# Three score buffers and a longer pipeline in a sliding-window attention stage: P turned two steps and mixed three steps behind the scores

## The reference, cut to what matters

```python
def block_fn(args):                      # one block of 128 queries, keys of this and the previous block
    n, qb, kb, vb = args
    s = jnp.einsum('bqkgd,bskd->bkgqs', qb.astype(f32), kb.astype(f32)) * scale
    valid = band & ((n - 1) * BLOCK + kj >= 0)
    s = jnp.where(valid, s, -jnp.inf)
    m = jnp.maximum(jnp.max(s, axis=-1), sink)
    p = jnp.exp(s - m[..., None])
    denom = jnp.sum(p, axis=-1) + jnp.exp(sink - m)
    o = jnp.einsum('bkgqs,bskd->bqkgd', p / denom[..., None], vb.astype(f32))
    return o.astype(hn.dtype)
...
return o @ w_o + b_o                     # then h = h + this
```

## Time and profile before

| what | value |
|---|---|
| three runs, median | 1072.28 us (1071.91 to 1072.68) |
| the profiled execution | 1071.9 us |
| its span, first to last instruction | 1070.1 us |
| busy over the span | PE 96%, DVE 55%, ACT 21%, POOL 66% |
| chain that ended last | PE 84%, DVE 8%, issue 3%, ACT 2% |
| attention, scores(0) to the last mix | 579 to 679 us |

### The profile page before, as it was taken

The page is one execution under the profiler, slowest core; times in us unless marked ns, Lnnn a source line. Parts: engine busy times, 40 slices in busy tenths (PEclk is TensorE's granted clock), DMA queues, the critical chain, the costliest instruction groups (busy, mean ns, idle before and its releaser), DMA issues.

```text
span 1070.1 us, 15713 instructions
## 1 busy us (share of the span) xinstructions
PE 1032.4 (96%) x5734; PEld 847.5 (79%) x5734; DVE 585.5 (55%) x688; ACT 224.0 (21%) x489; POOL 702.1 (66%) x563
## 2 busy tenths in 40 slices
PE   4889999999999999999999998999999999999996
PEld 1778888888888888888888676888888888888886
DVE  7998246587515613722865787478771372174125
ACT  4673211111000000100321777321110010010011
POOL 7997776597766766766656230488776676676660
PEclk9699999999999999999999999999999999999998
DMA  6113332222322222222222110132322222232212
GB/s 244 28 32 100 107 111 98 85 99 99 99 98 99 98 98 95 90 97 96 94 99 84 55 40 21 40 118 99 104 95 98 98 98 98 99 98 99 98 59 79
DMA packets 35888, 97.52 MB, mean 91 GB/s; under 512 B 11136, under 2 KB 13696, under 8 KB 35584
## 3 DMA queue, kind: packets, MB, share of 16 engines
q1 hardware_dynamic: 35840, 96.85, 27.3%
HBM read 92.37 MB, written 2.10 MB: 88 GB/s over the span
## 4 chain that ended last, share of the span: by engine, by line
PE 84%; DVE 8%; issue 3%; ACT 2%; POOL 1%; DMA 1%; DVEq 0%; SPq 0%
PE ps L1162 24%; PE ps L1163 23%; PE ps L1164 23%; PE ps L1126 2%; PE ps L1128 2%; PE ps L1127 2%; PE ps L1303 1%; PE ps L1317 1%; PE ps L1291 1%; ACT s_sb L597 1%; PE ps L1225 1%; PE ps L1224 1%; PE ps L1223 1%; DMA prm<-prm_in 1%; DVE hid L827 0%
## 5 line engine op out<-in xcount | busy, mean ns | idle before, releaser
L420 POOL TENSOR_TENSOR w_lo<-raw,w_hi 128x1024 fp32r<-128x1024 f32 x164 | 414.8, 2529 | 13.7
L1162 PE MATMUL ps<-hid,w_hi 128*128 128x512 f32 x704 | 275.8, 392 | 0.0
L1163 PE MATMUL ps<-hid,w_hi 128*128 128x512 f32 x704 | 274.0, 389 | 0.0
L1164 PE MATMUL ps<-hid,w_lo 128*128 128x512 f32 x704 | 274.0, 389 | 0.0
L344 POOL TENSOR_TENSOR gate_sb<-gate_sb 128x1 f32<-128x1 f32 x164 | 40.2, 245 | 315.9 <-PE ps L1164 276.3
L1162 PE MATMUL ps<-act,w_hi 128*128 128x512 f32 x464 | 180.6, 389 | 0.0
L1164 PE MATMUL ps<-act,w_lo 128*128 128x512 f32 x464 | 180.5, 389 | 0.0
L1163 PE MATMUL ps<-act,w_hi 128*128 128x512 f32 x464 | 180.5, 389 | 0.0
L417 POOL TENSOR_SCALAR w_hi<-raw 128x1024 fp32r<-128x1024 f32 x164 | 172.7, 1053 | 0.0
L1162 PEld LDWEIGHTS ps<-hid,w_hi 128*128 128x128 f32 x704 | 132.1, 188 | 30.9 <-issue 3.2
L1164 PEld LDWEIGHTS ps<-hid,w_lo 128*128 128x128 f32 x704 | 132.2, 188 | 27.7
(11 more groups left out here) (211 smaller groups left out, 1097.5 us busy)
## 6 DMA issues: line engine op xcount, KB each, us to landing
raw<-panels_in SPq DMA_DIRECT2D x164, 512.0 KB, 3.3
xy<-xu_in SPq DMA_DIRECT2D x4, 512.0 KB, 7.6
out<-h SPq DMA_DIRECT2D x8, 256.0 KB, 2.2
prm<-prm_in SPq DMA_DIRECT2D x1, 1280.0 KB, 5.5
h<-x_rows_in SPq DMA_DIRECT2D x1, 1280.0 KB, 13.2
h<-x_rows_in SPq DMA_DIRECT2D x1, 768.0 KB, 7.8
dd<-dd_in SPq DMA_DIRECT2D x1, 256.0 KB, 5.8
toep<-k_even SPq DMA_DIRECT2D x4, 64.0 KB, 2.3
```

The costliest lines, as they stand in the source:

```text
L420: nc.gpsimd.tensor_tensor(w_lo[:, s, :], raw[:, s % 2, :], w_hi[:, s, :].bitcast(F32), ALU.subtract).then_inc(w_split, 1)
L1162: mm(ps[:, bank, :], w_hi[:, s, w], x[:, 0, k, :], start=(k == 0), stop=False)
L1163: mm(ps[:, bank, :], w_hi[:, s, w], x[:, 1, k, :], start=False, stop=False)
L1164: last = mm(ps[:, bank, :], w_lo[:, s, w], x[:, 0, k, :], start=False, stop=(k == KT - 1))
```

## The change

- `s_sb` and the small tiles beside it (`mx`, `negm`, `den`, `rden`) get three buffers (`DEEP = 3`), taken in turn by Q % 3.
- TensorE turns P two steps behind the scores and mixes three behind. ScalarE's `turned` and `o_hi` move to lags 3 and 4, and `o_hi` stands ahead of `turned`. VectorE's `turned` and `o_low` move to lags 3 and 4, and `o_low` moves from behind `maxima` to ahead of `denominators`.
- o of even and odd quads lies in the two halves of bank 6. `mix(Q)` now waits for the `o_low` of Q - 1.
- Bank 7, now free, takes W_o's unit 2, which waits for a `stat_a` value reached before attention begins. The table `beside` is written anew: nine matmuls in each of steps 12 to 15, none in step 11, 12 in steps 16 and 17, 6 in step 18; TensorE has one step more.

```diff
+DEEP = 3
+OUT_BANK = (2, 3, 7, 1, 2, 3, 0, 1)
...
-        s_sb = sb("s_sb", [P, 2, 4, 2 * BLK + 1], where=over)
+        s_sb = sb("s_sb", [P, DEEP, 4, 2 * BLK + 1], where=over)
         mask = sb("mask", [P, 2 * BLK], where=over)
-        mx = sb("mx", [P, 2, 4], where=over)
-        negm = sb("negm", [P, 2, 4], where=over)
-        den = sb("den", [P, 2, 4], where=over)
-        rden = sb("rden", [P, 2, 4], where=over)
+        mx = sb("mx", [P, DEEP, 4], where=over)
+        negm = sb("negm", [P, DEEP, 4], where=over)
+        den = sb("den", [P, DEEP, 4], where=over)
+        rden = sb("rden", [P, DEEP, 4], where=over)
...
             def exps(Q):
-                u, n, q = Q // NBLK, Q % NBLK, Q % 2
+                u, n, r = Q // NBLK, Q % NBLK, Q % DEEP
                 a.wait_ge(m_step, 3 * Q + 3)
                 at = slice(window(n).start, 2 * BLK + 1)
                 for j in range(4):
-                    act_fn(s_sb[:, q, j, at], s_sb[:, q, j, at], ACT.Exp, bias=negm[:, q, j:j + 1],
-                           accum_out=den[:, q, j:j + 1]).then_inc(p_exp, 1)
+                    act_fn(s_sb[:, r, j, at], s_sb[:, r, j, at], ACT.Exp, bias=negm[:, r, j:j + 1],
+                           accum_out=den[:, r, j:j + 1]).then_inc(p_exp, 1)
...
-                       ps[:, 6 + q, 0:256].rearrange("p (t n) -> p t n", t=2),
+                       ps[:, 6, q * 256:(q + 1) * 256].rearrange("p (t n) -> p t n", t=2),
                        ACT.Copy).then_inc(ot_hi, 1)
 
-            skewed([(turned, 2), (o_hi, 3), (norm_p, 1), (exps, 0)])
+            skewed([(o_hi, 4), (turned, 3), (norm_p, 1), (exps, 0)])
...
-            skewed([(turned, 2), (denominators, 1), (maxima, 0), (o_low, 3), (next_queries, 0)])
+            skewed([(turned, 3), (o_low, 4), (denominators, 1), (maxima, 0), (next_queries, 0)])
 
 
             for m in range(KT):
                 v.wait_ge(unit_done, U_O + 1 + m)
-                stt(h[:, m, :], ps[:, (m + 2) % 4, :], COLS("b_o")[:, m:m + 1], h[:, m, :],
+                stt(h[:, m, :], ps[:, OUT_BANK[m], :], COLS("b_o")[:, m:m + 1], h[:, m, :],
...
             def out_unit(m, tiles):
 
-                free = ((bank_free, U_O + m + 3), (bank_free, U_O + m + 3), (s_masked, QUADS * NBLK),
+                free = ((bank_free, U_O + m + 3), (bank_free, U_O + m + 3), (stat_a, STAT_A[1]),
                         (s_masked, QUADS * NBLK))[m]
                 wait(pe, ot_lo, NBLK * (tiles[-1] // 2 + 1))
-                unit(U_O + m, m, hid[:, 1], None, tiles, bank=(m + 2) % 4, free=free)
+                unit(U_O + m, m, hid[:, 1], None, tiles, bank=OUT_BANK[m], free=free)
...
             def turn_p(Q):
-                u, n, q = Q // NBLK, Q % NBLK, Q % 2
+                u, n, r = Q // NBLK, Q % NBLK, Q % DEEP
                 pe.wait_ge(p_norm, 4 * Q + 4)
                 wait(pe, pt_a, Q)
                 wait(pe, pt_v, Q)
                 for j in range(4):
                     for b in halves_of(n):
                         at = (j % 2) * 2 * BLK + b * BLK
-                        last = turn(ps[:, 4 + j // 2, at:at + BLK], s_sb[:, q, j, b * BLK:(b + 1) * BLK], ident)
+                        last = turn(ps[:, 4 + j // 2, at:at + BLK], s_sb[:, r, j, b * BLK:(b + 1) * BLK], ident)
...
-                wait(pe, ot_lo, Q - 1)
+                wait(pe, ot_lo, Q)
                 halves = halves_of(n)
                 for t in range(2):
                     for b in halves:
                         for e in range(2):
                             kvh = 2 * (u // 2) + e
-                            last = mm(ps[64 * e:64 * e + 64, 6 + q, t * BLK:(t + 1) * BLK],
+                            last = mm(ps[64 * e:64 * e + 64, 6, (2 * q + t) * BLK:(2 * q + t + 1) * BLK],
                                       v_sb[:, n - 1 + b, kvh * HD:(kvh + 1) * HD], pT[:, q, 2 * e + t, b, :],
                                       start=(b == halves[0]), stop=(b == 1))
                 last.then_inc(o_mm, 1)
...
-            early, middle = range(0, 4), range(4, 6)
             beside = {Q: [(query_unit, 2 + (Q + 1) // 2, first_half if Q % 2 else second_half)]
                       for Q in range(2 * (KT - 2) - 1)}
             last_quad = QUADS * NBLK - 1
-            beside[last_quad - 4] = [(out_unit, 0, early)]
-            beside[last_quad - 3] = [(out_unit, 1, early)]
-            beside[last_quad + 1] = [(out_unit, 2, early), (out_unit, 0, middle)]
-            beside[last_quad + 2] = [(out_unit, 3, early), (out_unit, 1, middle)]
+
+            beside[last_quad - 3] = [(out_unit, 0, range(0, 3))]
+            beside[last_quad - 2] = [(out_unit, 0, range(3, 4)), (out_unit, 1, range(0, 2))]
+            beside[last_quad - 1] = [(out_unit, 1, range(2, 4)), (out_unit, 2, range(0, 1))]
+            beside[last_quad] = [(out_unit, 2, range(1, 4))]
+            middle = range(4, 6)
+            beside[last_quad + 1] = [(out_unit, 0, middle), (out_unit, 1, middle)]
+            beside[last_quad + 2] = [(out_unit, 3, range(0, 4))]
+            beside[last_quad + 3] = [(out_unit, 2, middle)]
 
             def dense(Q):
                 for work, m, tiles in beside.get(Q, []):
                     work(m, tiles)
 
-            skewed([(scores, 0), (dense, None), (mix, 2), (turn_p, 1)])
-
-            out_unit(2, middle)
+            skewed([(scores, 0), (dense, None), (mix, 3), (turn_p, 2)])
+
             out_unit(3, middle)
             for m in range(4):
                 out_unit(m, range(6, KT))
             for m in range(4, KT):
-                unit(U_O + m, m % 4, hid[:, 1], bank=(m + 2) % 4)
+                unit(U_O + m, m % 4, hid[:, 1], bank=OUT_BANK[m])
```

More of the change, by code:

```diff
@@ L596, in exps @@
                 for j in range(4):
-                    act_fn(s_sb[:, q, j, at], s_sb[:, q, j, at], ACT.Exp, bias=negm[:, q, j:j + 1],
-                           accum_out=den[:, q, j:j + 1]).then_inc(p_exp, 1)
+                    act_fn(s_sb[:, r, j, at], s_sb[:, r, j, at], ACT.Exp, bias=negm[:, r, j:j + 1],
+                           accum_out=den[:, r, j:j + 1]).then_inc(p_exp, 1)
             def norm_p(Q):
-                u, n, q = Q // NBLK, Q % NBLK, Q % 2
+                u, n, r = Q // NBLK, Q % NBLK, Q % DEEP
                 a.wait_ge(rden_done, Q + 1)
                 for j in range(4):
-                    act_fn(s_sb[:, q, j, window(n)], s_sb[:, q, j, window(n)], ACT.Copy,
-                           scale=rden[:, q, j:j + 1]).then_inc(p_norm, 1)
+                    act_fn(s_sb[:, r, j, window(n)], s_sb[:, r, j, window(n)], ACT.Copy,
+                           scale=rden[:, r, j:j + 1]).then_inc(p_norm, 1)
             def turned(Q):
@@ L981, in maxima @@
             def maxima(Q):
-                u, n, q = Q // NBLK, Q % NBLK, Q % 2
+                u, n, r = Q // NBLK, Q % NBLK, Q % DEEP
                 sink = COLS("sink")[:, 4 * u:4 * u + 4]
-                ts(s_sb[:, q, :, 2 * BLK:], sink.unsqueeze(2), 1.0, None, ALU.mult).then_inc(m_step, 1)
+                ts(s_sb[:, r, :, 2 * BLK:], sink.unsqueeze(2), 1.0, None, ALU.mult).then_inc(m_step, 1)
                 v.wait_ge(s_mm, Q + 1)
-                tt(s_sb[:, q, :, window(n)],
+                tt(s_sb[:, r, :, window(n)],
                    ps[:, 0:2, :].rearrange("p e (t m) -> p (e t) m", t=2)[:, :, window(n)],
@@ L991, in maxima @@
                 v.wait_ge(m_step, 3 * Q + 1)
-                nc.vector.tensor_reduce(mx[:, q], s_sb[:, q, :, window(n).start:], AX.X, ALU.max).then_inc(m_step, 1)
+                nc.vector.tensor_reduce(mx[:, r], s_sb[:, r, :, window(n).start:], AX.X, ALU.max).then_inc(m_step, 1)
                 v.wait_ge(m_step, 3 * Q + 2)
-                ts(negm[:, q], mx[:, q], -1.0, None, ALU.mult).then_inc(m_step, 1)
+                ts(negm[:, r], mx[:, r], -1.0, None, ALU.mult).then_inc(m_step, 1)
             def denominators(Q):
-                u, n, q = Q // NBLK, Q % NBLK, Q % 2
+                u, n, r = Q // NBLK, Q % NBLK, Q % DEEP
                 v.wait_ge(p_exp, 4 * Q + 4)
-                nc.vector.reciprocal(rden[:, q], den[:, q]).then_inc(rden_done, 1)
+                nc.vector.reciprocal(rden[:, r], den[:, r]).then_inc(rden_done, 1)
             def turned(Q):
```

## The result

Over 14 runs each, the changed kernel takes 1075.44 us (1073.69 to 1077.08) and the kernel before 1072.59 us (1071.31 to 1074.70): a ratio of 1.0028, 95% interval 1.0020 to 1.0036, so some 3 us slower. The forecast was 1075.6. The profiled execution took 1076.09 us. Code after the new constants has moved down by two lines: what was L994 is L996, L1317 is L1319, L420 is L422.

A forecast was written before the change was run, and what follows sets the result against it. TensorE was taken as the bound, but held negms and the longer VectorE-ScalarE loop move mix(15) from 677.82 to 682.54; less 1.36 for six matmuls, 3.4 us on the median 1072.28 gives 1075.6 (1070.9 to 1077.2).

The forecast's parts named there:

- The place and the lock: Attention: negm of quads 4, 6, 8, 10 held to the end of POOL's subtraction; mix(8) then idles TensorE 4.1 us.
- The loop: VectorE and ScalarE, exps to exps: o_low ahead of rden lengthens it by 0.63, from 4.97 to 5.60 us.
- The halved bank: mix's stricter wait, for o_low(Q-1) instead of o_low(Q-2), costs nothing by itself.
- The half clock: TensorE after step 11's idle: any slow clock is hidden by 1.1 us and 0.6 us in hand; cost taken 0.
- The tail: TensorE from mix(13) to mix(15): mixes, turns, twelve and six dense matmuls with switches, 8.66 us.
- Rival 3: Steps 12 to 15: nine dense matmuls cover the loop, empty step 11 costs nothing: 1067.7 us, chance 0.10.
- Rivals 1 and 2: negm(10) arrives before POOL's L420: 1073.3 us, chance 0.15; negm(4) and all others pass: 1071.1 us, chance 0.15.
- Rival 4: Half clock falls where no wait absorbs it, at most 1.6 us more: 1077.2 us, chance 0.05.

The follow-up runs named there:

- e1: Changed kernel with the maximum negated by the reduction itself, so negm as an operation of its own is gone: 1070.16 us, ratio 0.9978.
- e9: Changed kernel with negm from the negated reduction, sink copy as a reduction, query tile scaled in and read from PSUM: 1065.27 us, ratio 0.9941.
- e3: Kernel before with only the new order: o_hi ahead of turned, o_low ahead of denominators: 1078.08 us, ratio 1.0047.
- e5: Changed kernel with only deeper lags and three buffers kept; two banks for o, old orders, early tiles in steps 11 and 12: 1072.42 us, ratio 1.0000.
- e7: Changed kernel with VectorE's o_low put back behind maxima, the single bank for o kept: 1082.88 us, ratio 1.0084.
- e11: e5 with negated reduction, sink copy as reduction and query tile from PSUM, early matmuls spread 6, 6, 6, 3, 3 over steps 11 to 15: 1064.86 us.
- e6: Changed kernel with 12 dense matmuls in step 11 and six in each of steps 12 to 15: 1075.28 us, ratio 1.0017.
- e12: Kernel before with all three forms: negm by negated reduction, sink copy as reduction, query tile scaled in PSUM: 1071.87 us, ratio 0.9978.
- e10: e9 with the dense table of e6 (12 matmuls in step 11, six in each of steps 12 to 15): 1064.79 us, ratio 0.9935.
- e2: e1 with the sink copy into s_sb also written as a reduction, over one element: 1068.42 us, ratio 0.9961.

## Why the prediction was right

**The place and the lock: right.** scores(4) was forecast at 600.01 and started at 599.94; negm(4) at 605.29, inside a subtraction of 605.04 to 607.4, and stood at 605.20 in one of 604.98 to 607.33. exps(4), (6), (8) and (10) were forecast at 607.5, 619.96, 631.96 and 644.5 and started at 607.40, 619.86, 631.89 and 644.46. mix(4) waits 1.14 (1.16), mix(8) 4.10 (4.1). e1 shows the hold as the cause: with negm's own operation gone, 5 us come back. Not all of that is the hold, since the loop is shorter by the operation too: about 0.8 us, five loops behind exps(10) at 5.57 less the 5.41 of e9 (exps from 655.09 to 660.50 in its timeline).

**The loop: right.** o_low ahead of rden gives 2.72 from exps to rden (2.74), and the late loop is 5.57 (5.60) where it was 4.97. e3 shows that the order alone costs 5 us in the kernel before, holds and longer loop together; e5, that lags without order and halved bank cost nothing within 1.5 us.

**The halved bank: half right.** In the order given its stricter wait costs next to nothing, as forecast: o_low ends last ahead of mix(4) and mix(8), pT in the full steps, within 0.2 of each other. That is read from the trace alone; no run has the new orders with two banks. But I called it free by itself, and e7 shows that it is so only in that order; and e11, with two banks and the old orders, is no worse than e9.

**The half clock: the step that failed.** "A half clock after the idle of step 11 would be hidden by the 1.1 us that TensorE waits in step 12 and the 0.6 it has in hand at mix(13)." It came, for 4.2 us, and was not quite hidden. mix(9) stands at 654.25, where the loop allowed 650.02 + 2.88 = 652.90; at the full clock's prices (0.59, 1.02, 0.64 and 2.29 behind 647.41) it would have been ready at 651.95. So turned P(10) is late; VectorE's `turned` (656.40, after 1.92 of waiting) stands ahead of o_low and rden, which come at 657.01 and 657.34. exps(12) to exps(13) took 5.64 where 5.17 was due, and mix(13) stood at 674.32, 0.4 after the forecast. I had asked whether TensorE had time in hand, not whether VectorE's queue had. That the clock costs this much is worked out from the starts of one trace. That of e6, which has no half clock and the same dense work ahead of mix(15), agrees: scores(0) to mix(15) takes 102.80 us, 0.5 less; the run times can't resolve it.

**The tail: 0.4 too long.** From mix(13) to mix(15) I added 8.66; it took 8.24. The term that was too large is the switch into dense work. I had read it behind scores, 0.25 each time, and charged it behind turned P too, where twelve dense matmuls took 2.76 (not 2.97) and six 1.39 (not 1.61). The two misses cancel, and that mix(15) stands at 682.56 against 682.54 is luck. By the median the loss is 2.9 us, by the profiled spans 3.4; the interval, 2.1 to 3.9 us, holds both.

**The rivals.** Rival 3, that the nine dense matmuls cover the loop, was to be decided by exps(10) before 640.3. In the changed kernel it came at 644.46, so the rival is out. Once nothing on VectorE is held, e9 starts exps(10) at 634.52, and the change is worth 4 us (e9 against e12), where the rival had 4.6. So its price was about right for that kernel, but not its reason: `o_low` still stands ahead of the reciprocal in e9, and the loop is 5.41. Rivals 1 and 2 needed negm(10) or negm(4) to pass the split; neither did. Rival 4's price was 1.6; by the starts the clock cost some 0.4 on the way.

**Where the gain went.** Two by two:

| ratio to before | old forms | three forms |
|---|---|---|
| before | 1 | 0.9978 |
| after | 1.0028 | 0.9941 |

With the three forms the change brings 0.9941 / 0.9978 = 0.996, 4 us; with the old forms it costs 3. The traces agree: from scores(0) to mix(15) e9 takes 671.71 - 578.43 = 93.28 us, less the 1.36 of the six matmuls that it has more ahead 91.92, where e12 takes 95.80, 3.9 us more. The forms bring 2.4 us before and 9.3 after. The change does what it should for TensorE, and moves small operations of VectorE under POOL's long ones, which costs more. What stays open: how much of the 4 us is the pipeline's depth and how much the table, since I ran no kernel with the old lags and the new table.

The best of these, e9, e10 and e11, stand at 0.9932 to 0.9941, 6 to 7 us better than before, and can't be told apart.

## What to carry to other kernels

When VectorE and GpSimd work side by side, look at the longest, not the mean, of VectorE's smallest operations: a schedule that shifts them by 1 us can put each of them under a 2.4 us instruction, and here that turned 4 us won into 3 lost. Before a schedule is changed, give such operations a form that isn't held (folded into a reduction, or read from PSUM); then the schedules can be compared on their merits. When a wait of the bound engine disappears, follow every queue of the loop that set it, not the bound engine alone.

## What the hardware showed beyond that

- The hold didn't depend on the operation's size: 4 elements a partition took up to 2.30 us (e3) and 512 took 2.50 (e2), ending 0.03 and 0.29 us after POOL's instruction. The form did matter: a reduction to four values took 0.13 to 0.16 at all 16 places in e9, and tensor_scalar from PSUM 0.42 in the middle of a subtraction. The query tile's last step, a tensor_scalar of 512 elements, took 0.75 at all 8 places in e9, read from PSUM, and 0.49 to 1.38 in the kernel before, read from SBUF.
- A reduction with the negation in it took 1.22 us, as long as without, so the negation added no time.
- The granted clock fell to 0.50 behind a wait of 4.10 us (and was 0.53 in the 3.6 us behind e2's of 2.32), and stayed at 1.00 behind e6's waits of 1.19 and 1.65.
